# One hybrid encoder block on one core: one wait removed, and several steps of VectorE, ScalarE and TensorE reordered

## The chip, the cores and the metric

The kernel runs on one core of a Trainium2 chip. The metric is the device time of one execution in microseconds (us). Before the change three runs took 961.53 to 962.06 us, median 961.74 us.

## The reference, cut to what matters

One input, x (512 tokens by 1024 channels), is RMS-normalised and multiplied by one large input projection. Three branches use slices of it: A, a chunkwise mLSTM with 4 heads; B, sparse attention, in which an indexer scores all keys for each query and the best 128 are attended by 8 heads; M, cross-attention into 256 memory tokens with 4 heads. Each branch is gated, projected, merged with sigmoid gates and projected once more.

```python
kv_m = rms_norm(mem, mem_norm_g) @ w_mem_kv             # start of the kernel
score = (relu(qi . ki / 8) * wi).sum(heads)             # indexer of branch B
score = where(admissible, score, -inf)
_, idx = lax.top_k(score, 128)                          # top_k = min(256, S // 4)
s = q . k[idx] / sqrt(128); p = softmax(s); o = p @ v[idx]
y_b = o * silu(z_b)
merged = g0 * (y_a @ w_branch[0]) + g1 * (y_b @ w_branch[1]) + g2 * (y_m @ w_branch[2])
out = x + merged @ w_out
```

## The kernel before, in words

**Precision.** Every float32 operand of a large product is split into a high part (a rounded copy made by ScalarE) and a low part (the remainder, made by VectorE with one subtraction); TensorE then runs three passes, high by high, high by low and low by high. So each block of weights has a cast on ScalarE (`split_hi`, `b_high`) and a subtraction on VectorE (`split_lo`, `b_low`) before TensorE may use it. All engines run written-out programs of their own and meet through semaphores; within an engine the order is exactly the order of the code.

**The start.** SP, the queue that issues the loads, sends alternately tiles of `mem` (`load_mem`) and pieces of the first weight panel (`load_piece`). After memory half 0, piece 0, memory half 1 and piece 1 it waits until memory half 0 has landed (`mem_landed[0]`), and goes on with pieces 2, 3 and 4.

**Top-k.** Query tile 0 needs no selection. For tiles 1, 2 and 3 VectorE takes the 8 largest scores of each row and replaces them, 16 times per tile: one such round is `top_round(t)` (MAX8 and MATCH_REPLACE8). The rounds fill VectorE's time from the M stage to the first head pair of B. In all, four rounds of tile 1 and eight of tile 2 stand behind the last panel of M. `make_masks` then turns the marked scores into an additive mask for attention.

**Branch B, head pairs.** `b_unit(i)` on TensorE computes queries, keys and values of head pair i for all tokens with a Strassen-like scheme of seven products (`b_product`, numbers 0 to 6), each 24 matmuls, accumulating in four PSUM banks. VectorE empties or combines banks with `b_add(i, 1)`, `b_add(i, 3)` and `b_add(i, 5)`, each two additions that raise `u_added`; ScalarE saves others with `b_save` and, after product 6, with `b_last_copy`, which raises `u_read`. Product 6 accumulates in banks 0 and 1 and waits at each for the matching half of `b_add(i, 3)` (`u_added`, 6i + 3 and 6i + 4). Then come two `f_panel`s, whose first block in bank 0 waits for `u_read`, that is for `b_last_copy`. On ScalarE `b_last_copy(i)` stands behind `b_values_high(r)`, which waits for all six additions of the pair (`u_added`, 6i + 6). GpSimd squares queries and keys (`b_squares`) behind the same six additions. VectorE's `b_rotary` sums those squares, applies the rotation and raises `b_rotated`, for which the transposes `b_turn_qk` wait. With r = 2i and l = 2i + 1 for the two heads of the pair, head r is attended within the two f_panels and head l within the next pair's unit. VectorE's order is `b_body`, ScalarE's the `b_body` of its own.

**The tail of B.** For the last pair both heads are attended in the first three of four branch panels (`branch_panel(q)`, 8 blocks or slots each: four banks for the first half of K, four for the second). The hooks of a slot (a step of attention) run before that slot's matmuls and before its wait for the bank. Panel q + 1 may write bank b only when VectorE has read what panel q left there: `branch_merge(q, b)` raises `bank_empty[b]`. The chain of one head is `b_turn_qk` (TensorE), `b_qk_high` (ScalarE), `b_qk_low` (VectorE), `b_score` (TensorE), `b_maxes` (VectorE), `b_exps` (ScalarE), `b_scale_p` (VectorE), `b_turn_p` (TensorE), `b_probs_high` (ScalarE), `b_probs` (VectorE), `b_values` (TensorE), `b_finish` (VectorE).

Lines used below: `top_round` L2392, `make_masks` L2468, `b_low` L2483, `b_add` L2490, `b_rotary` L2526 to L2543, `b_values_low` L2555, `b_qk_low` L2547 and L2549, `b_finish` L2522, `branch_merge` L2668, `yb_low` L2661, `m_rest` L2431, `b_high` L1691, `b_values_high` L1719, `z_evac` L1750, `b_squares` L3055, `b_turn_qk` L1094, `b_score` L1105, `b_turn_p` L1113, `b_values` L1123, `b_product` L1141, panels L781.

## Time and profile before

| what | value |
|---|---|
| median of 3 runs | 961.74 us |
| the profiled execution, its own time | 962.06 us |
| its span in the trace | 960.0 us |
| TensorE matmuls busy | 954.0 us (99%) |
| VectorE busy | 707.4 us (74%) |
| ScalarE busy | 535.2 us (56%) |
| GpSimd busy | 346.1 us (36%) |

Times in rows are microseconds from the span's start. PE is TensorE, DVE VectorE, ACT ScalarE, POOL GpSimd, SPq the queue of SP. A busy TensorE is not one at its peak, since its matmuls overlap; the share of 99% says that it hardly ever stood still.

### The profile page before, as it was taken

The numbers are of one execution on the slowest core, as the hardware profiler recorded it, in microseconds if no ns is written. First come the engines' busy times: TensorE is split into PE (matmuls) and PEld (weight loads), VectorE is DVE, ScalarE is ACT, GpSimd is POOL, SyncE is SP. The second block draws the span as 40 slices with busy tenths as digits, with TensorE's granted clock in tenths as the row PEclk, the third lists the DMA queues.
The fourth block names the chain that finished last, engine by engine and source line by source line (L and its number), as shares of the span: only waits on it lengthen the run. The fifth ranks groups of instructions, "written<-read, shape, count | busy, mean of one in ns | idle before, by whom it ended". The sixth has DMA issues, their size and how long they took to land.

```text
span 960.0 us, 13409 instructions
## 1 busy us (share of the span) xinstructions
PE 954.0 (99%) x4897; PEld 839.3 (87%) x4897; DVE 707.4 (74%) x1079; ACT 535.2 (56%) x810; POOL 346.1 (36%) x247
## 2 busy tenths in 40 slices
PE   9999999999999999999999999999999999999998
PEld 7888888888989988988988888898998989988887
DVE  6878987688996676686687565895766958634586
ACT  6877644465456456546573422585765857732251
POOL 0200834456327137136120081362714527107500
PEclk9999999999999999999999999999999999999999
DMA  8624222144531531531354335616043150738312
GB/s 283 245 88 132 89 88 73 58 132 132 166 97 56 176 111 43 155 112 64 121 207 153 122 110 163 221 34 197 1 138 93 33 154 1 258 92 312 125 45 87
DMA packets 105156, 119.27 MB, mean 124 GB/s; under 512 B 4772, under 2 KB 80136, under 8 KB 104332
## 3 DMA queue, kind: packets, MB, share of 16 engines
q1 hardware_dynamic: 105084, 118.53, 38.1%
q8 instruction: 34, 0.56, 0.2%
q14 instruction: 22, 0.18, 0.1%
q10 hardware_dynamic: 16, 0.00, 0.0%
HBM read 106.45 MB, written 12.07 MB: 123 GB/s over the span
## 4 chain that ended last, share of the span: by engine, by line
PE 95%; DVE 3%; DMA 1%; ACT 1%; issue 1%; SPq 0%; DVEq 0%; ACTq 0%
PE proj L781 42%; PE proj L1141 12%; PE proj L1290 9%; PE att L1311 7%; PE proj L1311 5%; PE att L1361 3%; PE proj L951 2%; PE att L1105 2%; PE att L1123 2%; PE att L1070 1%; PE proj L1247 1%; PE att L1113 1%; PE att L1048 1%; PE att L1094 1%; DVE score L2397 1%; PE att L1247 1%
## 5 line engine op out<-in xcount | busy, mean ns | idle before, releaser
L781 PE MATMUL proj<-hT_hi,w_hi 128*128 128x512 f32 x328 | 129.0, 393 | 0.0
L781 PE MATMUL proj<-hT_hi,w_lo 128*128 128x512 f32 x328 | 128.0, 390 | 0.0
L781 PE MATMUL proj<-hT_lo,w_hi 128*128 128x512 f32 x328 | 127.8, 390 | 0.0
L2132 DVE TENSOR_TENSOR w_lo<-w_raw,w_hi 128x2048 fp32r<-128x2048 f32 x28 | 68.5, 2447 | 52.9 <-ACT w_hi L1411 48.9
L1411 ACT ACTIVATE w_hi<-w_raw 128x2048 fp32r<-128x2048 f32 x28 | 53.6, 1914 | 73.2 <-PE proj L781 71.7
L781 PE MATMUL proj<-y_hi,w_hi 128*128 128x512 f32 x192 | 75.2, 392 | 0.7 <-ACT arena L1750 0.7
L781 PE MATMUL proj<-y_hi,w_lo 128*128 128x512 f32 x192 | 74.8, 390 | 0.0
L781 PE MATMUL proj<-y_lo,w_hi 128*128 128x512 f32 x192 | 74.7, 389 | 0.0
L781 PEld LDWEIGHTS proj<-hT_hi,w_lo 128*128 128x128 f32 x328 | 61.6, 188 | 13.1
L781 PEld LDWEIGHTS proj<-hT_lo,w_hi 128*128 128x128 f32 x328 | 61.6, 188 | 12.3
L781 PEld LDWEIGHTS proj<-hT_hi,w_hi 128*128 128x128 f32 x328 | 61.6, 188 | 12.2
L3024 POOL TENSOR_TENSOR w_raw<-merged,w_raw 128x384 f32<-128x384 f32 x32 | 36.2, 1167 | 54.3 <-DVE w_lo L2483 31.6
L2726 DVE TENSOR_TENSOR w_lo<-w_raw,w_hi 128x1536 fp32r<-128x1536 f32 (+1 forms) x21 | 35.9, 1709 | 21.9 <-ACT w_hi L1919 21.9
L1919 ACT ACTIVATE w_hi<-w_raw 128x1536 fp32r<-128x1536 f32 (+1 forms) x21 | 29.1, 1385 | 40.6 <-DMA w_raw<-w_in_in 12.9
L3096 POOL TENSOR_TENSOR w_raw<-merged,w_raw 128x384 f32<-128x384 f32 x32 | 40.3, 1307 | 29.5 <-DVE w_lo L2726 29.5
L781 PEld LDWEIGHTS proj<-y_hi,w_hi 128*128 128x128 f32 x192 | 36.1, 188 | 8.5 <-ACT sig L1750 1.1
L781 PEld LDWEIGHTS proj<-y_hi,w_lo 128*128 128x128 f32 x192 | 36.0, 188 | 7.5
L781 PEld LDWEIGHTS proj<-y_lo,w_hi 128*128 128x128 f32 x192 | 36.1, 188 | 7.4
L2738 DVE SCALAR_TENSOR_TENSOR negmask<-proj,small,negmask 128x511 f32<-128x511 f32 (+2 forms) x48 | 35.5, 747 | 4.0 <-ACT negmask L1952 2.8
L1290 PE MATMUL proj<-hT_hi,w_hi 128*128 128x512 f32 x96 | 37.7, 392 | 0.0
L1290 PE MATMUL proj<-hT_hi,w_lo 128*128 128x512 f32 x96 | 37.4, 390 | 0.0
L1290 PE MATMUL proj<-hT_lo,w_hi 128*128 128x512 f32 x96 | 37.4, 390 | 0.0
(522 smaller groups left out, 2924.0 us busy)
## 6 DMA issues: line engine op xcount, KB each, us to landing
w_raw<-w_in_in SPq DMA_DIRECT2D x36, 512.0 KB, 4.5
w_raw<-w_in_in SPq DMA_DIRECT2D x56, 256.0 KB, 3.7
w_raw<-w_branch_in SPq DMA_DIRECT2D x10, 1024.0 KB, 7.6
merged<-w_in_in SPq DMA_DIRECT2D x38, 256.0 KB, 3.7
merged<-w_in_in SPq DMA_DIRECT2D x14, 512.0 KB, 5.9
w_raw<-w_in_in SPq DMA_DIRECT2D x6, 1024.0 KB, 5.3
w_raw<-w_mem_kv_in SPq DMA_DIRECT2D x10, 512.0 KB, 6.8
yF<-x_in SPq DMA_DIRECT2D x8, 512.0 KB, 7.5
```

The lines of the kernel that those rows point to most:

```text
L781: ins = mm(ps, lhs[a](k, k0), rhs[b](k, k0), start=(first and k == 0 and j == 0), stop=(last and k == KH - 1 and j == 2))
L1141: ins = mm(to[t][:, 0:UNIT_N], lhs[a](k, t), w[b][:, k, :], start=(start and k == 0 and j == 0), stop=(k == KH - 1 and j == 2), skip_group ...
L1290: ins = mm(banks[b][:, :], w[a][:, k, e * P:(e + 1) * P], hT[b_][:, kh * KH + k, :], start=(kh == 0 and k == 0 and j == 0), stop=(kh == 1 ...
L1311: ins = mm(to[t][:, 0:UNIT_N], lhs[a](k, t), w[b][:, k, :], start=(start and k == 0 and j == 0), stop=(k == KH - 1 and j == 2), skip_group ...
L1361: ins = mm(to[t][:, :], lhs[a](k, t), w[b][:, k, :], start=(start and k == 0 and (a, b) == (0, 0)), stop=(k == KH - 1 and (a, b) == parts[ ...
L1411: A_(w_hi[:, kh, :, 0:n], w_raw[:, kh, :, 0:n], ACT.Copy).then_inc(w_hi_done, 1)
L1919: A_(operand(op_hi, n), raw_of(n, first), ACT.Copy).then_inc(op_high, 1)
L2132: V.tensor_tensor(w_lo[:, kh, :, 0:n], w_raw[:, kh, :, 0:n], w_hi[:, kh, :, 0:n].bitcast(F32), ALU.subtract).then_inc(w_lo_done, 1)
L2726: V.tensor_tensor(operand(op_lo, n), raw_of(n, first), operand(op_hi, n).bitcast(F32), ALU.subtract)\
L2738: ins = V.scalar_tensor_tensor(acc[:, lag:], u[:, 0:S - lag], hcw[:, CONV - 1 - lag, b:b + 1], acc[:, lag:], ALU.mult, ALU.add)
L3024: ins = G.tensor_tensor(b_w[out][:, at], b_w[left][:, at], b_w[right][:, at], op)
L3096: ins = G.tensor_tensor(dst[:, at], left[:, at], right[:, at], ALU.subtract)
```

## The change

On SP the wait for memory half 0 goes. On TensorE the attention hooks of the tail move to earlier slots. On ScalarE `b_probs_high` moves ahead of the next panel's cast for both heads, and one cast moves behind `b_qk_high(l)`. On VectorE, two rounds of tile 2 ahead of `m_rest` and two ahead of pair 0 go, and four more stand within pair 0: one more ahead of `b_low(4)`, and four ahead of `b_add(0, 3)` where one stood behind it; `make_masks` moves ahead of `b_add(0, 5)`; `b_values_low(r)` of the last pair moves up; the order of the tail changes. On GpSimd one wait of `b_squares` names `b_rotated` in place of `b_vlow`.

```diff
             load_mem(1)
             load_piece(1, 0, 0)
-            sp.wait_ge(mem_landed[0], 16)
             load_piece(2, 0, 0)
...
-            branch_panel(0, y_split(1), {1: [lambda: b_score(r)], 6: [lambda: b_turn_p(r)]})
-            branch_panel(1, None, {0: [lambda: b_values(r)], 1: [lambda: b_turn_qk(l)], 3: [lambda: b_score(l)],
-                                   6: [lambda: b_turn_p(l)]})
-            branch_panel(2, y_split(2), {0: [lambda: b_values(l)]})
+            branch_panel(0, y_split(1), {1: [lambda: b_score(r)], 5: [lambda: b_turn_p(r)], 7: [lambda: b_values(r)]})
+            branch_panel(1, None, {0: [lambda: b_turn_qk(l)], 2: [lambda: b_score(l)], 5: [lambda: b_turn_p(l)],
+                                   7: [lambda: b_values(l)]})
+            branch_panel(2, y_split(2))
...
             b_exps(r)
+            b_probs_high(r)
             split_hi(GB[0] + 1, 0, GB[1] + 2, 512)
-            b_probs_high(r)
-            split_hi(GB[0] + 1, 1, GB[1] + 2, 512, (3, GB[2][3] + 1))
             b_values_high(l)
             b_qk_high(l)
+            split_hi(GB[0] + 1, 1, GB[1] + 2, 512, (3, GB[2][3] + 1))
             b_exps(l)
+            b_probs_high(l)
             split_hi(GB[0] + 2, 0, GB[1] + 3, 512)
-            b_probs_high(l)
...
-                rounds(2, 1)
+                rounds(2, 2)
                 b_low(n + 4)
...
                 if i:
                     b_finish(tail)
+                rounds(2, 4)
                 b_add(i, 3, (banks[0], banks[1]), b_fifth, 5)
-                rounds(2, 1)
                 b_low(n + 7)
+                if i == 0:
+                    make_masks()
                 b_add(i, 5, (banks[2], banks[3]), b_second, 3)
                 b_low(n + 8)
                 b_rotary(r)
+                b_values_low(r)
                 if last:
                     return
-                b_values_low(r)
-                if i == 0:
-                    make_masks()
...
             b_low(0)
-            for _ in range(2):
-                top_round(2)
             m_rest(M_HEADS - 1)
             bs_low_of(3, 4)
             b_low(1)
-            for _ in range(4):
+            for _ in range(2):
                 top_round(2)
...
             split_lo(GB[0], 0, 512)
-            b_values_low(r)
             b_qk_low(r)
+            b_rotary(l)
             split_lo(GB[0], 1, 512)
             b_maxes(r)
             for k in range(4, KT):
                 ym_low(k)
-            b_rotary(l)
             b_scale_p(r)
+            b_probs(r)
             split_lo(GB[0] + 1, 0, 512)
-            b_probs(r)
+            b_finish(r)
+            b_values_low(l)
+            b_qk_low(l)
             for b in range(4):
                 branch_merge(0, b)
             split_lo(GB[0] + 1, 1, 512)
-            b_finish(r)
-            b_values_low(l)
-            b_qk_low(l)
             b_maxes(l)
             b_scale_p(l)
+            b_probs(l)
             split_lo(GB[0] + 2, 0, 512)
-            b_probs(l)
-            for b in range(2):
-                branch_merge(1, b)
+            b_finish(l)
             for k in range(KH):
                 yb_low(k)
-            for b in range(2, 4):
+            for b in range(4):
                 branch_merge(1, b)
             split_lo(GB[0] + 2, 1, 512)
-            b_finish(l)
...
-                    pool.wait_ge(b_vlow, a)
+                    pool.wait_ge(b_rotated, a)
```

## Rows read from the trace of the kernel before

**Rows 1.** The page: busy time, and the granted clock in 40 slices.

```profile
PE 954.0 (99%) x4897; PEld 839.3 (87%) x4897; DVE 707.4 (74%) x1079; ACT 535.2 (56%) x810; POOL 346.1 (36%) x247
...
PEclk9999999999999999999999999999999999999999
```

**Rows 2.** Waits of TensorE: for whom, us in total, times, longest.

```profile
PE proj L781 <- ACT arena L1750: 0.7, 1, 0.7
PE proj L951 <- ACT w_hi L1462: 0.6, 1, 0.6
```

**Rows 3.** SP's waits up to 30 us; then ScalarE's timeline (start, duration).

```profile
SPq L519 <- DMA merged<-mem_in: 1.0, 1, 1.0
...
7.68 0.63 ACT L1462 ACTIVATE w_hi<-w_raw 128x512 fp32r<-128x512 f32 x1 [2.08 <-DMA w_raw<-w_mem_kv_in]
```

**Rows 4.** Timeline of VectorE, from the end of M to the first pair.

```profile
226.77 0.69 DVE L2431 TENSOR_TENSOR yF<-att,arena 128x512 f32<-128x512 f32 x1 [0.75 <-PE att L1070]
...
232.99 0.55 DVE L2395 MAX8 small<-score 128x8 f32<-128x384 f32 x1
...
237.98 1.76 DVE L2483 TENSOR_TENSOR w_lo<-w_raw,w_hi 128x1536 fp32r<-128x1536 f32 x1
239.66 0.42 DVE L2395 MAX8 small<-score 128x8 f32<-128x256 f32 x1
...
243.59 1.83 DVE L2483 TENSOR_TENSOR w_lo<-w_raw,w_hi 128x1536 fp32r<-128x1536 f32 x1
...
251.68 3.43 DVE L2483 TENSOR_TENSOR w_lo<-merged,w_hi 128x1536 fp32r<-128x1536 f32 x2
255.03 1.01 DVE L2490 TENSOR_TENSOR merged<-proj,merged 128x384 f32<-128x384 f32 x2
255.96 0.55 DVE L2395 MAX8 small<-score 128x8 f32<-128x384 f32 x1
```

**Rows 5.** Timeline of ScalarE in the first pair.

```profile
235.76 1.49 ACT L1691 ACTIVATE w_hi<-w_raw 128x1536 fp32r<-128x1536 f32 x1
...
260.07 0.40 ACT L1719 ACTIVATE b_vh<-yF 128x256 fp32r<-128x256 f32 x1
...
260.69 0.49 ACT L1703 ACTIVATE arena<-proj 128x384 f32<-128x384 f32 x1
```

**Rows 6.** TensorE in the first pair: its timeline, then the chain of waits.

```profile
258.42 0.33 PE L1141 MATMUL proj<-w_hi,hT_hi 128*128 128x384 f32 x1
...
233.52 29.22 PE proj L1141 x168
...
270.94 0.87 PE att L1094 x8
```

**Rows 7.** Timeline of GpSimd, first pair.

```profile
259.97 1.04 POOL L3055 TENSOR_TENSOR arena<-yF 128x512 f32<-128x512 f32 x1 [16.16 <-DVE yF L2490]
```

**Rows 8.** Timeline of VectorE behind the first pair's additions.

```profile
263.56 1.22 DVE L2526 TENSOR_REDUCE small<-arena 128x8 f32<-128x1024 f32 x1 [0.94 <-POOL arena L3055]
...
268.75 0.69 DVE L2541 TENSOR_TENSOR arena<-arena,small 128x512 f32<-128x512 f32 x1
...
270.37 0.17 DVE L2469 MEMSET negmask<- 128x128 f32 x1
...
273.26 1.76 DVE L2483 TENSOR_TENSOR w_lo<-merged,w_hi 128x1536 fp32r<-128x1536 f32 x1
```

**Rows 9.** The chain of waits in the tail: start, us, what.

```profile
523.05 2.79 PE proj L781 x12
525.84 0.87 PE att L1094 x8
```

**Rows 10.** Timeline of VectorE in the tail.

```profile
517.04 1.28 DVE L2668 TENSOR_TENSOR merged<-proj,tabs 128x512 f32<-128x512 f32 x2
...
527.61 0.68 DVE L2549 TENSOR_TENSOR b_kl<-att,b_kh 128x512 fp32r<-128x512 f32 x1
...
545.93 2.49 DVE L2661 TENSOR_TENSOR y_lo<-yF,y_hi 128x512 fp32r<-128x512 f32 x4
```

## The prediction, made before the changed kernel was run

> **What bounds the kernel now.** I read the page's busy times first: TensorE's matmuls cover 954.0 of 960.0 us, while VectorE, the next, covers 74% [rows 1]. Then TensorE's waits: the only two that this change could reach are 0.7 us, before the first branch panel, and 0.6 us, at the start [rows 2]. So TensorE's own program is the bound, in order and all but gapless. Two things follow. A reordering can gain at most about 1.5 us, whatever it does for other engines. And every us for which TensorE is newly made to stand is a us at the end, because nothing later gives it back. The question is therefore not what the moved steps cost, but whether any of them now arrives after TensorE needs it. I walk the new orders through with the durations of the timelines, stage by stage.
>
> **The start.** SP stood 1.0 us for memory half 0 [rows 3]. Without that, pieces 2 to 4 go out up to 1.0 us sooner. What TensorE waits for there is piece 1, issued before the wait either way; ScalarE casts it at 7.68 after 2.08 us of waiting for its landing [rows 3]. The removal can help piece 1 by nothing direct; the sooner transfers may disturb it or, if the transfers behind it let the group finish sooner, spare the stall. Bounds: below, the whole 0.6 us stall goes, with some 0.2 us of small gaps beside it; above, piece 1 is later by the whole 1.0 us by which its successors are sooner, and by as much again through memory half 1, +2.0 us. I take 0: the 256 KB in question is already on its way. The Trainium skill (DMA: Bandwidth & Descriptors, Queues, rings and completion order) says that each transfer engine takes up the descriptors of one ring in order, but that a later one may finish first. By the first half of that the removal costs 0; no row shows the order within a ring.
>
> **The first pair, VectorE.** Four rounds of tile 2 take 4.99 us (232.99 to 237.98), 1.25 each; four rounds of tile 1 take 3.93 us (239.66 to 243.59); one `b_low` takes 1.68 us (two in 3.35, 251.68 to 255.03); the two halves of a `b_add` 0.93 us (255.03 to 255.96) [rows 4]. The change shifts rounds from where VectorE would only wait to where it is late. The two rounds ahead of `m_rest` go, but `m_rest` waits for TensorE until 226.77 anyway [rows 4], so the time is lost and 232.99 stays. From there: two rounds, to 235.48. `b_low(2)` needs ScalarE's cast, which ends at 235.76 + 1.49 = 237.25 [rows 5]: another 1.8 us idle. `b_low(2)` to 238.97, four rounds of tile 1 to 242.90, `b_low(3)` to 244.6, `b_add(0, 1)` to 245.5, two rounds to 248.0, `b_low(4)` to 249.7, two rounds to 252.2, `b_low(5)` and `b_low(6)` to 255.5. Up to here TensorE just gets what it needs: the seven products take 29.22 us, 4.17 each, and the last starts at 258.42 [rows 6], so product 4 at 250.1 and product 5 at 254.26 find their operands 0.3 us ready. Now four rounds, 4.99 us, stand ahead of `b_add(0, 3)`: 260.5. Its first half ends at 261.05. Product 6 wants it at 258.42. **First stall: 261.15 - 258.42 = 2.7 us.**
>
> **Behind it.** `b_add(0, 3)` ends at 261.45, `b_low(7)` at 263.1. `make_masks` now stands here: 273.26 - 270.37 = 2.9 us [rows 8], to 266.0; then `b_add(0, 5)`, its last half landing at 267.0 (before: 259.9, which released ScalarE at 260.07 [rows 5]). ScalarE's `b_values_high(0)` waits for that, and `b_last_copy(0)` is queued behind it: 0.62 us of copies (260.07 to 260.69), then 0.49 [rows 5], to 268.2. The f_panel's first block needs bank 0 from that copy. It wanted to start when product 6 ends, at 258.42 + 4.17 + 2.7 = 265.3, and starts at 268.3. **Second stall: 3.0 us.** GpSimd's squares start with the same addition: 267.1 in place of 259.97 [rows 7]; they then took until 263.56 [rows 7, 8], so 3.6 us, to 270.7. The rotation takes from 263.56 to 268.75 + 0.69 = 269.44 [rows 8], 5.9 us, so `b_rotated` comes at 276.6. The transposes, at 270.94 before [rows 6], are due at 276.6 too. I add 0.1 us. VectorE then has 2.9 us less left to do than before, since the masks are made, and stays ahead. Later pairs have the same orders as before, except that GpSimd's squares of head l start about 0.9 us sooner: nothing waits for them. Stage sum +5.8 us. Bounds: if the rounds ran 10% faster and every semaphore cost nothing, about 1.5 us less; if `b_low(8)`, which runs beside the squares, slows them as it did at its worst, and products 4 and 5 are late as well, 1 us more.
>
> **The tail, head r.** `b_values_low(r)` moving up by 5 us and `b_rotary(l)` moving ahead of the second half of the panel's split delay that split and `ym_low(4)` to `(7)` to about 508.7. The fifth slot of panel 0 needs them at 509.2: hidden with 0.5 us to spare, and a loss of at most as much if GpSimd's squares, now at the same time, slow VectorE. `b_turn_p(r)` and `b_values(r)`, one slot sooner (2.7 us), find probabilities and their low parts ready by about 2 us. But the merges of panel 0 have moved. Before, VectorE did them from 517.04 [rows 10], ahead of panel 1 at 523.05 [rows 9]. Now they stand behind `b_qk_low(l)`, which waits for ScalarE's copies of `b_turn_qk(l)`, which TensorE does only in the first slot of panel 1, at 523.05. Bank 0 is needed right after those transposes. From the rows of before: transposes at 525.84 [rows 9], VectorE's last `b_qk_low` at 527.61 and its next instruction 0.6 us on, 528.2 [rows 10]: 2.4 us. Add a merge, 0.69, and the signal: 3.15 us after the transposes' start, of which they take 0.87. **Third stall: 2.3 us.**
>
> **The tail, head l.** The merges of panel 1 now stand behind `b_finish(l)` and four `yb_low`. `b_values(l)` is the hook of the last slot, so its result is there 2.74 us before panel 2 wants bank 0. Behind it VectorE does `b_finish` (0.6), four `yb_low` (2.4 us by [rows 10]) and one merge (0.69): 3.75 us with the signal. **Fourth stall: 1.1 us.** The 0.7 us wait for `z_evac` [rows 2] stays: nothing ahead of it on ScalarE changes. Bounds of the two together: nothing, if an operand I think late comes early, to 4.5 us, if `b_scale_p` or the split of panel 2 is late too.
>
> **Sum.** 0 + 2.7 + 3.0 + 0.1 + 2.3 + 1.1 = 9.2 us. The profiled execution took 962.06 us (960.0 of it span), 0.3 above the median of 961.74. 962.06 + 9.2 = 971.3, and at the median's level 970.9 us, 1.0% slower.
>
> **Rivals.** First, **only one of the two places stalls.** If the tail's order works out (the ready times there rest on a longer walk), 970.9 - 3.4 = 967.5 us. If the first pair's works out, 970.9 - 5.8 = 965.1 us. For the first speaks the length of the walk, against it that a bank's wait behind a hook in the same slot can't be early. Chance of one of them 0.14.
>
> Second, **everything is covered, and the start gains.** VectorE arrives at `b_add(0, 3)` before 258.3, which takes 2.2 us off my walk, and at `b_add(0, 5)` before 264, and the merges come before 523. Then only the start is left, -0.6 us, or 961.1 us: no change. The point that decides is the 4.99 us of rounds against the 2.9 us that lie between `b_low(6)` at 255.5 and product 6 at 258.42. The rows leave no room for it: 0.04.
>
> Third, **the clock falls behind the stalls.** The granted clock is 2.4 GHz in all forty slices [rows 1], behind its 0.7 us wait too [rows 2]. Stalls of 2.7 and 3.0 us with 4.2 us of work between them are new, and no row shows what the clock does then. If it fell to 1.2 GHz for as long as one product (4.2 us at full speed), the product would take 4.2 us more: 975.1 us. Chance 0.07. The Trainium skill (TensorE: Matmul & The Clock Gate, Part 1: The HAM clock gate) says that the array falls to half its clock after idling and has to earn it back; the rows of before neither show nor exclude it for such gaps.
>
> Fourth, **the start gets worse** by the upper bound of 2.0 us through shared transfers, the rest as forecast: 972.9 us. Chance 0.08.
>
> **How the numbers follow.** The forecast has 0.67: 970.9 us, its own range 969 to 972.5. The range to hold 8 in 10 goes from 967 us (the tail works out) to 973.5 us (a bad start and a little more). A measurement can't tell less than 0.2% (1.9 us) from no change. Faster by more would need more than TensorE waits now: 0.01. Within 0.2%: 0.04, the second rival. Slower: 0.95.
>
> **What would show it.** TensorE's waits should list `proj` L1141 for VectorE's `b_add` (2.7 us, near 258), `proj` L781 for ScalarE near 265 (3.0 us), and `proj` L781 for VectorE's `branch_merge` twice in the tail, 2.3 us behind the transposes and 1.1 us at panel 2. TensorE's busy time should stay at 954 us. The prediction is wrong if the span grows by less than 4 us, or if the stalls stand elsewhere than at these four.

## The result, and the profile after

The changed kernel took 974.37 us (median of 4 runs, 972.04 to 976.38) against 961.75 (961.53 to 962.06) for the kernel before in the same session: a ratio of 1.013, with a 95% interval of 1.0107 to 1.0153. It is 12.6 us slower. The forecast was 9.2 us slower, 970.9 us; 974.37 lies above its whole range.

In the kernel after, lines of the functions above stand one to six lower than before: `b_product` L1140, panels L780, `b_add` L2489, `branch_merge` L2665, `b_low` L2482, `ym_low` L2654, `split_lo` L2131, `b_last_copy` L1702, `make_mask` (within `make_masks`) L2399, `b_values_low` L2554, `b_squares` L3049.

Its profiled execution took 974.56 us, of which 972.5 are span. From the page (busy time; clock in 40 slices), against [rows 1]:

```profile
PE 957.4 (98%) x4897; PEld 840.3 (86%) x4897; DVE 715.0 (74%) x1079; ACT 534.5 (55%) x810; POOL 341.4 (35%) x247
...
PEclk9999999999999999999999999999999999999999
```

The same 4897 matmuls, 3.4 us more of busy time, and 9 us more of standing still. The slices of 24 us hide what the clock did: their line is the same as that of the kernel before. TensorE's waits, which answer to [rows 2] (for whom, us in total, times, longest):

```profile
PE proj L780 <- DVE merged L2665: 3.3, 2, 2.2
PE proj L1140 <- DVE merged L2489: 2.8, 1, 2.8
PE proj L950 <- ACT w_hi L1461: 1.6, 1, 1.6
...
PE proj L780 <- DVE w_lo L2131: 1.4, 1, 1.4
PE proj L780 <- ACT arena L1702: 1.1, 1, 1.1
PE proj L780 <- DVE y_lo L2654: 0.4, 1, 0.4
PE proj L1140 <- DVE b_op_lo L2482: 0.2, 1, 0.2
```

Four of them are the four stalls that were forecast, at the places that were forecast: 2.8, 1.1, and the 3.3, which is 2.2 and 1.05. Of another size or new are 1.6 at the start (0.6 before), the 1.1, where 3.0 was forecast, 1.4 + 0.4 at the tail's first panel, where 0.7 of [rows 2] has gone, and 0.2 at product 4 of the first pair.

The start of TensorE's first long run of matmuls, in the kernel before and after:

```profile
8.36 0.50 PE L951 MATMUL proj<-w_hi,y_hi 128*128 128x512 f32 x1 [0.60 <-ACT w_hi L1462]
9.29 0.50 PE L950 MATMUL proj<-w_hi,y_hi 128*128 128x512 f32 x1 [1.58 <-ACT w_hi L1461]
```

The landmarks in TensorE's timeline after (start, duration, idle time before and for whom). 262.72 answers to 258.42 of [rows 6], 529.99 to 525.84 of [rows 9]:

```profile
262.72 0.41 PE L1140 MATMUL proj<-w_hi,hT_hi 128*128 128x384 f32 x1 [2.77 <-DVE merged L2489]
...
268.18 0.47 PE L780 MATMUL proj<-hT_hi,b_op_hi 128*128 128x512 f32 x1 [1.05 <-ACT arena L1702]
...
502.44 0.47 PE L780 MATMUL proj<-y_hi,w_hi 128*128 128x512 f32 x1 [1.38 <-DVE w_lo L2131]
...
515.92 0.47 PE L780 MATMUL proj<-y_hi,w_hi 128*128 128x512 f32 x1 [0.37 <-DVE y_lo L2654]
...
529.99 1.03 PE L1093 MATMUL att<-ident,arena 128*128 128x128 f32 x8
533.26 0.50 PE L780 MATMUL proj<-y_hi,w_hi 128*128 128x512 f32 x1 [2.23 <-DVE merged L2665]
533.60 0.39 PE L780 MATMUL proj<-y_lo,w_hi 128*128 128x512 f32 x1
...
534.84 0.63 PE L780 MATMUL proj<-y_hi,w_hi 128*128 128x512 f32 x1
535.27 0.63 PE L780 MATMUL proj<-y_lo,w_hi 128*128 128x512 f32 x1
...
563.04 0.47 PE L780 MATMUL proj<-y_hi,w_hi 128*128 128x512 f32 x1 [1.05 <-DVE merged L2665]
```

From 534.84 the matmuls start every 0.43 us instead of every 0.23. The granted clock of this stretch in 2 us steps (window; busy times of PE, PEld, DVE, ACT, POOL; then PEclk):

```profile
532.00:534.00 2.00, 0.74 (x3) 0.65 (x4) 2.00 (x5) 1.57 (x1) 0.00 (x0) 1.00 0.00 0
534.00:536.00 2.00, 2.00 (x7) 1.57 (x7) 2.00 (x3) 0.00 (x0) 0.00 (x0) 0.66 0.00 0
536.00:538.00 2.00, 2.00 (x6) 1.52 (x6) 1.19 (x1) 0.00 (x0) 0.00 (x0) 0.50 0.04 8
538.00:540.00 2.00, 2.00 (x10) 1.64 (x9) 0.00 (x0) 0.00 (x0) 0.00 (x0) 0.99 0.69 217
```

0.50 is the lower of the two levels, 1.2 GHz; 1.00 is the upper one, 2.4 GHz. Behind the 2.2 us wait the clock stood there for about 3.4 us ((1.00 - 0.66) x 2 / 0.5 + 2.0), in which 1.7 us of work was lost. Behind the 2.8 us wait of the same execution it stayed at 1.00.

The 12.5 us of span then come from: start +0.9 (the first long run of matmuls at 9.29 instead of 8.36); first pair +4.75 (the transposes at 276.62, in the chain of waits, instead of 270.94 [rows 6], less the 0.9; the waits of 2.8, 1.1 and 0.2 with their restarts make it up); the tail's first panel +1.2 (waits of 1.4 and 0.4 in place of 0.7, and one restart more); third stall 2.2 + 0.2; clock 1.7; fourth 1.1 + 0.2. That is 12.25; 0.25 is spread over small gaps. The 0.2 behind a wait is its restart. The second matmul starts 0.25 to 0.34 us after the first, where 0.17 and 0.23 are the rhythm; and a wait is counted from the end of the matmul before it, while in the rhythm the next one starts 0.16 us ahead of that end (0.39 - 0.23).

### The profile page after: what moved, and what is told of

Read it like the earlier page. It is cut to its first block, busy times and chain, and to the rows that moved or that the text cites. A ratio compares the mean times of both kernels' runs of the same rounds, so it can differ in the third digit from the quotient of the medians.

```text
span 972.5 us, 13407 instructions
## 1 busy us (share of the span) xinstructions
PE 957.4 (98%) x4897; PEld 840.3 (86%) x4897; DVE 715.0 (74%) x1079; ACT 534.5 (55%) x810; POOL 341.4 (35%) x247
## 4 chain that ended last, share of the span: by engine, by line
PE 87%; DVE 8%; issue 2%; ACT 1%; DMA 1%; POOL 0%; SPq 0%; DVEq 0%; ACTq 0%
PE proj L780 39%; PE proj L1289 9%; PE proj L1140 9%; PE att L1310 7%; PE proj L1310 5%; PE att L1360 3%; PE proj L950 2%; PE att L1122 2%; PE att L1104 1%; DVE score L2396 1%; PE att L1069 1%; DVE small L2394 1%; PE proj L1246 1%; PE att L1112 1%; PE att L1047 1%
## 5 line engine op out<-in xcount | busy, mean ns | idle before, releaser
L780 PE MATMUL proj<-hT_hi,w_hi 128*128 128x512 f32 x328 | 129.0, 393 | 0.0
L780 PE MATMUL proj<-hT_hi,w_lo 128*128 128x512 f32 x328 | 128.0, 390 | 0.0
L780 PE MATMUL proj<-hT_lo,w_hi 128*128 128x512 f32 x328 | 127.8, 390 | 0.0
L2131 DVE TENSOR_TENSOR w_lo<-w_raw,w_hi 128x2048 fp32r<-128x2048 f32 x28 | 68.9, 2462 | 49.6 <-ACT w_hi L1410 45.6
L780 PE MATMUL proj<-y_hi,w_hi 128*128 128x512 f32 x192 | 76.1, 397 | 5.0 <-DVE merged L2665 3.3
L780 PE MATMUL proj<-y_hi,w_lo 128*128 128x512 f32 x192 | 75.4, 393 | 0.0
L780 PE MATMUL proj<-y_lo,w_hi 128*128 128x512 f32 x192 | 75.4, 393 | 0.0
L780 PEld LDWEIGHTS proj<-hT_hi,w_lo 128*128 128x128 f32 x328 | 61.6, 188 | 13.1
L780 PEld LDWEIGHTS proj<-hT_lo,w_hi 128*128 128x128 f32 x328 | 61.7, 188 | 12.3
L780 PEld LDWEIGHTS proj<-hT_hi,w_hi 128*128 128x128 f32 x328 | 61.6, 188 | 12.2
L1918 ACT ACTIVATE w_hi<-w_raw 128x1536 fp32r<-128x1536 f32 (+1 forms) x21 | 29.1, 1385 | 40.5 <-DMA w_raw<-w_in_in 11.6
L3018 POOL TENSOR_TENSOR w_raw<-merged,w_raw 128x384 f32<-128x384 f32 x32 | 32.3, 1040 | 53.2 <-DVE w_lo L2482 29.7
L3090 POOL TENSOR_TENSOR w_raw<-merged,w_raw 128x384 f32<-128x384 f32 x32 | 40.3, 1303 | 29.5 <-DVE w_lo L2720 29.5
L780 PEld LDWEIGHTS proj<-y_hi,w_hi 128*128 128x128 f32 x192 | 36.4, 189 | 13.8 <-issue 4.0
L780 PEld LDWEIGHTS proj<-y_hi,w_lo 128*128 128x128 f32 x192 | 36.5, 190 | 7.8
L780 PEld LDWEIGHTS proj<-y_lo,w_hi 128*128 128x128 f32 x192 | 36.5, 190 | 7.4
```

What stands on the lines that cost most here:

```text
L780: ins = mm(ps, lhs[a](k, k0), rhs[b](k, k0), start=(first and k == 0 and j == 0), stop=(last and k == KH - 1 and j == 2))
L1918: A_(operand(op_hi, n), raw_of(n, first), ACT.Copy).then_inc(op_high, 1)
L2131: V.tensor_tensor(w_lo[:, kh, :, 0:n], w_raw[:, kh, :, 0:n], w_hi[:, kh, :, 0:n].bitcast(F32), ALU.subtract).then_inc(w_lo_done, 1)
L3018: ins = G.tensor_tensor(b_w[out][:, at], b_w[left][:, at], b_w[right][:, at], op)
L3090: ins = G.tensor_tensor(dst[:, at], left[:, at], right[:, at], ALU.subtract)
```

## The experiments

All times are medians of device times, each ratio with its 95% interval against the kernel before on the same chip (961.65 to 961.72 us in the four sessions). "Before +" means the kernel before with only that edit, "after +" the changed kernel with it.

### Which part costs what: b_start, b_pair, b_tail

**b_start**, before + only SP's wait gone:

```diff
             load_piece(1, 0, 0)
-            sp.wait_ge(mem_landed[0], 16)
```

> The kernel before with only the wait for memory half 0 taken away. My theory, from the two traces: the wait of TensorE for piece 1 grows from 0.6 to 1.6 us because pieces 2 to 4, issued 1.0 us sooner, share the transfer engines with piece 1; time +0.9 us (962.7), and piece 1 needs 6.4 us from issue to landing in place of 5.5. Rival: the later landing was chance of that one execution, time within 0.3 us of before.

Measured: 962.88 us, 1.0008 [0.9999, 1.0017]. The interval holds no change by a hair, and the ratio gives 0.8 us where the medians differ by 1.2. In the profile piece 1 is cast at 8.50 instead of 7.68, the first long run starts at 9.18 instead of 8.36, and the span is 0.7 us longer.

**b_pair**, before + only VectorE's edits in and ahead of pair 0:

```diff
-                rounds(2, 1)
+                rounds(2, 2)
                 b_low(n + 4)
...
+                rounds(2, 4)
                 b_add(i, 3, (banks[0], banks[1]), b_fifth, 5)
-                rounds(2, 1)
                 b_low(n + 7)
+                if i == 0:
+                    make_masks()
```

> The kernel before with only VectorE's changes around the first head pair (rounds and masks). My theory: TensorE waits 2.8 us for the first half of b_add(0, 3) and 1.1 us for b_last_copy(0), and the first pair's chain is 4.8 us late, time 966.5. By my prediction's step the second wait would be 3.0 us and the time 967.5. Rival: these waits exist only since the start is late by 0.9 us and the loads with it; then less than 3 us.

Measured: 966.76 us, 1.0058 [1.0044, 1.0071]. In the profiled execution the 2.8 us wait is there and the 1.1 us wait is not. Its clock in 5 us steps says why:

```profile
260.00:265.00 5.00, 3.95 (x16) 3.98 (x17) 4.90 (x11) 0.00 (x0) 0.00 (x0) 0.73 0.15 35
265.00:270.00 5.00, 5.00 (x24) 4.45 (x23) 3.07 (x3) 2.97 (x5) 3.48 (x2) 0.93 0.84 230
```

Here the low clock came behind the 2.8 us wait. It stretched product 6 by 1.7 us, and in that time `b_last_copy` arrived. The expected time, 966.5, came out although one of its two waits did not: the clock had taken its place.

**b_tail**, before + only the tail's edits (all hunks of the tail in the diff above, `b_values_low(r)` among them).

> The kernel before with only the edits of the tail (hooks, ScalarE's and VectorE's order, b_values_low of the last pair, GpSimd's wait). My theory: waits of 1.4 (in place of 0.7), 0.4, 2.2 and 1.1 us, so +4.7 us in waits and the matmuls that restart behind them, and a stretch of some 3.4 us at the lower clock behind the 2.2 us wait, another 1.7 us: 966.5 without and 968.2 with it. Rival: the clock falls only since the first pair has stalled TensorE before; then every execution shows 966.5 and a granted clock of 1.000.

Measured: 966.91 us, 1.0055 [1.0041, 1.0069], with waits of 3.3 (two), 1.4 and 0.4 us. Its profiled execution was the slowest of the five (968.69), and has two more waits that neither other profile has, 1.2 us near 32 and 0.4 near 47, far ahead of the tail; what brings them isn't shown. Four of its five executions had a mean clock of 1.000, so the tail costs about 5 us without any help of the clock: 1.2 + 2.4 + 1.3 by the profile of after. The three parts add up to 1.2 + 5.1 + 5.3 = 11.6 of 12.6 us; the rest, 1.0 us, is less than one low stretch of the clock costs, and whether it is that isn't shown.

### The tail's first panel: a_vlow, a_place

The forecast had the second half of the split and `ym_low` at 508.7, wanted at 509.2, and the first half in time. The first half came late by 1.4 us, and `ym_low` at the fifth slot by 0.4. VectorE in the tail after (start, duration):

```profile
494.95 1.31 DVE L2554 TENSOR_TENSOR b_vl<-yF,b_vh 128x256 fp32r<-128x256 f32 x1
496.19 1.25 DVE L2554 TENSOR_TENSOR b_vl<-merged,b_vh 128x256 fp32r<-128x256 f32 x1
497.37 2.48 DVE L2654 TENSOR_TENSOR y_lo<-merged,y_hi 128x512 fp32r<-128x512 f32 x4
499.78 2.28 DVE L2131 TENSOR_TENSOR w_lo<-w_raw,w_hi 128x2048 fp32r<-128x2048 f32 x1
```

and GpSimd at that time:

```profile
494.94 2.22 POOL L3049 TENSOR_TENSOR arena<-arena 128x512 f32<-128x512 f32 x2 [2.53 <-DVE arena L2540]
```

Each half of `b_values_low` takes 1.3 us instead of 0.42. Rival theories: the two engines get into each other's way, or the instructions are slow at this place. **a_vlow** is after + the old wait of the squares:

```diff
-                    pool.wait_ge(b_rotated, a)
+                    pool.wait_ge(b_vlow, a)
```

> The changed kernel with GpSimd's b_squares waiting for b_vlow again. My theory: in the last pair b_values_low took 2.4 us in place of 0.75 since GpSimd's squares ran beside it; without that, VectorE's split for panel 0 is 1.7 us sooner, TensorE's wait of 1.4 us there becomes the 0.7 us for z_evac, time 0.7 to 0.9 us below the changed kernel's median (973.5). Rival: the slow b_values_low comes from something else (its place in VectorE's queue), nothing changes.

Measured: 972.93 us, 1.0119 [1.0103, 1.0134]; the expectation of a shorter wait was missed: it stayed at 1.3 us. VectorE's timeline:

```profile
494.07 0.43 DVE L2554 TENSOR_TENSOR b_vl<-yF,b_vh 128x256 fp32r<-128x256 f32 x1
494.41 0.42 DVE L2554 TENSOR_TENSOR b_vl<-merged,b_vh 128x256 fp32r<-128x256 f32 x1
494.75 4.18 DVE L2654 TENSOR_TENSOR y_lo<-merged,y_hi 128x512 fp32r<-128x512 f32 x4
```

`b_values_low` is fast again (0.43 and 0.42 us), and the four `ym_low`, now beside the squares (495.00 to 497.78), take 4.18 us where they took 2.48. The delay is of the two engines together; the wait only chose who paid.

**a_place** is a_vlow + `b_values_low(r)` of the last pair back in the tail:

```diff
                 b_rotary(r)
-                b_values_low(r)
                 if last:
                     return
+                b_values_low(r)
...
             split_lo(GB[0], 0, 512)
+            b_values_low(r)
             b_qk_low(r)
```

> The changed kernel with GpSimd's wait on b_vlow and b_values_low(r) of the last pair back behind the first split of panel 0, so that the squares of head l run beside no two-input VectorE work on SBUF. My theory after a_vlow, where the 1.7 us only moved to the four ym_low: these, the split and b_values_low(r) then take their plain 2.4, 2.2 and 0.75 us, the split comes 2.4 us sooner, TensorE's wait of 1.4 us becomes the 0.7 us for z_evac: time 0.7 to 0.9 us below the changed kernel. Rival: GpSimd's overlap is no cause, the wait stays at 1.3 to 1.4 us.

Measured: 973.29 us, 1.0119 [1.0102, 1.0136], 1.1 us less than after. The 1.4 us wait is gone and the 0.7 us wait for `z_evac` back; four `ym_low` take 2.50 us, since the squares start only behind `b_values_low`. So by the waits the place of `b_values_low(r)` was worth 0.7 us. The medians can't tell it: with four runs that spread over 1.7 us a_place is 1.1 us below after and 0.4 above a_vlow. The 0.4 us wait at the fifth slot stays in both; in a_place VectorE stood 1.05 us for the squares, which now come late, ahead of `b_rotary(l)`, so what that wait would be without the squares isn't shown.

### The masks: a_masks, a_masks2, b_masks

The second stall was forecast at 3.0 us with 2.9 us for `make_masks` [rows 8]. After, it took 1.2 us (264.68 to 265.88):

```profile
264.68 0.17 DVE L2468 MEMSET negmask<- 128x128 f32 x1
264.88 0.90 DVE L2399 TENSOR_SCALAR negmask<-score 128x256 f32<-128x256 f32 x3
...
265.88 1.02 DVE L2489 TENSOR_TENSOR yF<-proj,yF 128x384 f32<-128x384 f32 x2
```

Of the kernel before, the row that [rows 8] left out, and GpSimd's at the same time:

```profile
270.57 2.59 DVE L2400 TENSOR_SCALAR negmask<-score 128x256 f32<-128x256 f32 x3
```

```profile
270.56 2.31 POOL L3055 TENSOR_TENSOR arena<-arena 128x512 f32<-128x512 f32 x2 [3.48 <-DVE b_vl L2555]
```

**a_masks** is after + the masks back at their old place:

```diff
-                if i == 0:
-                    make_masks()
                 b_add(i, 5, (banks[2], banks[3]), b_second, 3)
...
                 if last:
                     return
+                if i == 0:
+                    make_masks()
```

> The changed kernel with make_masks back behind b_values_low(r) of the first pair. My theory: the masks took 1.2 us ahead of b_add(0, 5) and 2.9 us only where GpSimd's squares run beside them. Without them there, b_last_copy(0) is 1.2 us sooner and TensorE's wait of 1.1 us for it goes; behind the rotation the masks or b_values_low take up to 2 us longer again beside the squares. Time 1.1 to 1.3 us below the changed kernel's 974.4. Rival, my prediction's step (the masks cost 2.9 us wherever they stand): 2.9 us or more below.

Measured: 974.24 us, 1.0121 [1.0104, 1.0138]. The wait for `b_last_copy` is gone, yet the time is not less. ScalarE's timeline shows that the masks were its cause: the first half of `b_last_copy` ends 4.05 us after product 6 has started (268.51 and 264.46), where it takes 5.31 in after (267.56 + 0.47, and 262.72), and product 6 takes 4.17. But here the clock fell behind the 2.8 us wait, and that stretched product 6 to 5.80 us, the same as in b_pair, a_vlow and a_place, where the masks stand at their new place and the 1.1 us wait is missing too. In after, with the wait and no slow clock there, the f_panel starts 5.46 us behind product 6. So in an execution whose clock falls there the masks cost nothing, and the low stretch costs only some 0.3 us more than the wait that it takes the place of. The mean clock of the profiled execution was 0.995: there were three low stretches (0.71 at 10 to 15 us, 0.66 at 265 to 270, 0.66 at 535 to 540), and the one of its four executions with a mean clock of 1.000 took 971.56 us. The masks still took 0.90 us at the old place, since `b_values_low` (1.31 + 1.26), ahead of them, met the squares, as it does in after. **a_masks2**, a_masks + the old wait of the squares (as in a_vlow), tells whether it was the place or the neighbour:

> The kernel a_masks (changed kernel, masks back behind b_values_low(r)) with GpSimd's wait on b_vlow again, so that the squares start with the masks. My theory, contention of VectorE and GpSimd: the masks take 2.9 us as in the kernel before, and b_values_low(r) 0.75 us in place of 2.5; time as a_masks. Rival: the masks are faster in the changed kernel for a reason of their own and keep their 1.2 us.

Measured: 973.88 us, 1.0127 [1.0112, 1.0143], and in VectorE's timeline:

```profile
273.75 0.42 DVE L2554 TENSOR_TENSOR b_vl<-yF,b_vh 128x256 fp32r<-128x256 f32 x1
274.10 0.42 DVE L2554 TENSOR_TENSOR b_vl<-merged,b_vh 128x256 fp32r<-128x256 f32 x1
274.49 0.17 DVE L2468 MEMSET negmask<- 128x128 f32 x1
274.69 2.58 DVE L2399 TENSOR_SCALAR negmask<-score 128x256 f32<-128x256 f32 x3
```

The same three instructions, 2.58 us with the squares beside them (274.68 to 276.99) and 0.90 without, at the same place. **b_masks** takes the step alone, before + the masks ahead of `b_add(0, 5)`:

```diff
                 b_low(n + 7)
+                if i == 0:
+                    make_masks()
                 b_add(i, 5, (banks[2], banks[3]), b_second, 3)
```

> The kernel before with only make_masks moved ahead of b_add(0, 5). My theory: 1.2 us there, b_last_copy(0) starts at 261.8 and frees bank 0 at 262.3, before the f_panel wants it at 262.6; b_rotated comes at 270.6, wanted at 270.9: time as before, within 0.3 us. Rival, the step of my prediction (2.9 us): bank 0 at 264.0 and b_rotated at 272.3, so 1.4 us slower.

Measured: 961.74 us, 1.0000 [0.9991, 1.0009]; masks 0.90 us, no new wait of TensorE. Moving the masks is free by itself. On top of the rounds it brings the 1.1 us wait, in an execution whose clock stays high there.

### The rounds: a_rounds

After + the four rounds behind the addition:

```diff
-                rounds(2, 4)
                 b_add(i, 3, (banks[0], banks[1]), b_fifth, 5)
+                rounds(2, 4)
```

> The changed kernel with the four rounds of tile 2 behind b_add(0, 3) in place of ahead of it. My theory: TensorE's 2.8 us wait at product 6 goes, but VectorE reaches b_add(0, 5) no sooner, so ScalarE's b_last_copy(0) comes at the same time and the whole wait, some 4.4 us, stands before the first f_panel block: time within 0.5 us of the changed kernel. Rival (each wait has its own cause): 2.8 us less.

Measured: 976.53 us, 1.0162 [1.0145, 1.0179]. The 2.8 us wait is gone and this one has come:

```profile
PE proj L780 <- ACT arena L1702: 4.1, 1, 4.1
```

5 us of rounds moved from one side of `b_add(0, 3)` to the other stay ahead of `b_add(0, 5)`, and the stall moves to where that one is waited for: 4.1 instead of 2.8 + 1.1. The expectation of the same time within 0.5 us was missed by the median, 2.2 us above after, with intervals that overlap. The mean clocks, 0.993 to 0.998 (0.9953 in the mean, 0.9970 in after; each 0.001 is 1 us), account for 1.7 of it. The cost is in the number of rounds ahead of the pair's last addition, not in their place.

### The merges: a_merge

After + the four `branch_merge(0, b)` ahead of `b_finish(r)`:

```diff
             split_lo(GB[0] + 1, 0, 512)
+            for b in range(4):
+                branch_merge(0, b)
             b_finish(r)
             b_values_low(l)
             b_qk_low(l)
-            for b in range(4):
-                branch_merge(0, b)
```

> The changed kernel with the four branch_merge(0, b) ahead of b_finish(r). My theory: the 2.2 us wait of panel 1 behind the transposes goes, the one of 1.1 us at panel 2 stays: 2.3 us less, 972.1, and in executions where the clock fell behind that wait another 1.7 us less. Rival: b_qk_low(l), now behind the merges, is late instead and TensorE waits the same time at b_score(l).

Measured: 969.74 us, 1.0081 [1.0065, 1.0098], 4.6 us less than after. Its only wait for merges is the fourth:

```profile
PE proj L780 <- DVE merged L2665: 1.0, 1, 1.0
```

2.2 + 0.2 us of wait and 1.7 us of clock are gone, 4.1 together; near 530 the matmuls run at 0.23 us each. From the transposes of head l to the end of the span the two profiled executions take 442.5 us (after, from 529.99) and 438.3 (from 530.62): 4.2 less. In that execution of after a stall forecast at 2.3 us was worth nearly twice that, because the clock fell behind it. It doesn't always: of the seven profiled executions with the 2.2 us wait the clock fell behind it in four (after, a_place, a_masks, a_masks2), and not in a_vlow, a_rounds and b_tail.

The profiled execution of a_merge shows something else too. Behind its 2.8 us wait the clock was low for 6.8 us (0.59 at 261 to 262, 0.50 in each us from there to 268), twice as long as in the others; its f_panel starts 7.05 us behind product 6 instead of 5.46.

### What a stall costs: c_short, c_long

Two waits made on purpose ahead of the last branch panel, for casts that are done a few us late there:

```diff
-            branch_panel(3, None)
+            branch_panel(3, None, {0: [lambda: pe.wait_ge(w_hi_done, 2 * (GB[0] + 3) + 2)]})
```

c_long waits for `w_lo_done` instead.

> The kernel before, with TensorE made to wait once, ahead of branch panel 3 (a stretch without any other wait), until ScalarE has cast the panel's second half: one clean wait of 2.0 us (cast 1.92 us behind the end of panel 2). My theory: such a wait costs itself and 0.2 us for the matmuls that restart, 963.9, and in some executions a stretch at the lower clock behind it, 1.7 us more. Rival: the clock falls only where several waits lie close together; then every execution shows a granted clock of 1.000 and 963.9.

> The same with the wait ended by VectorE's subtraction behind the cast, so one wait of 4.3 us (1.92 + 2.3 + signals). My theory: 4.5 us for the wait and, now in every execution, 1.7 us of lower clock: 967.9, granted clock 0.998. Rival: 966.2 at 1.000.

Measured: c_short 965.82 us, 1.0040 [1.0024, 1.0055], for one wait of 2.1 us. Its clock:

```profile
574.00:576.00 2.00, 0.92 (x2) 0.83 (x3) 1.97 (x2) 0.98 (x1) 2.00 (x1) 0.73 0.41 125
576.00:578.00 2.00, 2.00 (x6) 1.53 (x5) 1.97 (x3) 0.00 (x0) 1.92 (x2) 0.50 0.16 16
```

In this execution (966.40 us) 2.1 + 0.2 + 1.7 = 4.0 of 4.7 us. Two of four had a mean clock of 0.998 (966.40 and 965.88), two of 1.000 (965.75 and 964.55). So the four don't separate cleanly by the clock; its 1.7 us is read from the profile. c_long took 972.98 us, 1.0121 [1.0105, 1.0136]. Its wait was 8.8 us where 4.3 was expected: I had overlooked that VectorE's split stands behind the merges of panel 2. The clock was low from about 575 to 585, some 6 us of it in the wait (which began at 572.6), where it costs nothing, and 4 us (581.3 to 585.3) behind it, which cost 2.0: 8.8 + 2.0 + 0.2 of 11.3 us. All four executions had a mean clock of 0.995.

The mean clocks of all runs show how often the clock was low anywhere in an execution. With a wait of 2.1 or 2.2 us as the longest (c_short, b_tail) 3 of 9 executions were below 1.000; with the 2.8 us wait, in most with the 2.2 us one as well (b_pair, after, a_vlow, a_place, a_masks, a_masks2, a_merge), 29 of 30; with 4.1 us (a_rounds) all 4; with 8.8 all 4; with none of them (b_start, b_bank, b_masks, b_swap, s_late) none of 55. Where it fell only the profiled executions tell: behind the 2.8 us wait in six of seven (not in after), behind the 4.1 us wait, behind the 2.2 us wait in four of seven. One low stretch, in a_masks from about 9.5 to 12.9, stands behind a start wait of only 1.3 us.

### The start, and the wait that was there before: b_swap, s_late, b_bank

```diff
-            load_mem(1)
             load_piece(1, 0, 0)
+            load_mem(1)
             sp.wait_ge(mem_landed[0], 16)
```

is **b_swap**; **s_late** waits for `piece_landed[0]` in the place of `mem_landed[0]`, which is later.

> The kernel before with weight piece 1 issued ahead of memory half 1. My theory: piece 1 is 0.47 us sooner in the queue and TensorE's 0.6 us wait for its cast shrinks to 0.1 or 0.2 us, while memory half 1, wanted at 7.1 us, still lands in time: 0.4 us faster. Rival: memory half 1 is late instead, same time or slower.

> The kernel before with SP waiting for weight piece 0 in place of memory half 0, so that pieces 2 to 5 are issued some 1.4 us later than before and 2.4 us later than with the change. My theory (sooner successors delay piece 1): piece 1 lands sooner than its 5.5 us from issue, by about as much as it was later in the changed kernel, some 4.6 us, and TensorE's wait for its cast goes; ScalarE then waits 1.4 us longer for pieces 2 and 4, which may cost TensorE up to 1 us. Rival: piece 1's landing does not depend on what is issued behind it, the 0.6 us wait stays and the later pieces come on top.

Measured: b_swap 961.45 us, 1.0002 [0.9993, 1.0011]; s_late 962.09 us, 1.0002 [0.9993, 1.0011]: no difference to be told. In both the wait for piece 1 went, and others of 0.2 and 0.4 us came; the 0.4 us that b_swap was expected to gain did not show. What they do show is when piece 1 lands, read from the start of ScalarE's cast of it. With successors held until piece 0 had landed (s_late, one execution): 6.51. Held until memory half 0 had landed (before, b_pair, b_tail, b_bank, b_masks, c_short, c_long): 6.70 to 7.68, mean 7.3. Not held (b_start, after and the six variants of after): 7.60 to 8.61, mean 8.1. The kernels before and after were each profiled at the late end of their group. Of after, where [rows 3] have 7.68:

```profile
8.61 0.63 ACT L1461 ACTIVATE w_hi<-w_raw 128x512 fp32r<-128x512 f32 x1 [3.03 <-DMA w_raw<-w_mem_kv_in]
```

**b_bank** is before without the early wait on bank 1, whose release comes from `z_evac`; the matmuls' own waits still guard the bank:

```diff
-            pe.wait_ge(bank_empty[1], BF[2][1] + 2 * PAIRS - 1)
```

> The kernel before without TensorE's early wait for bank 1 ahead of the branch panels (the panel's own wait, ahead of the block that writes bank 1, has the same value). The 0.7 us wait ends with ScalarE's evacuation of bank 1, while the first block needs bank 0, free 0.1 us before the f_panel ends. My theory: the wait goes, 0.7 to 0.9 us faster, 960.9, and faster than both kernels. Rival: the next wait of the same chain (the split of the panel's second half, which ScalarE does behind that evacuation) takes its place; no change.

Measured: 961.01 us (960.58 to 961.18, 11 runs), 0.9993 [0.9984, 1.0002]. The 0.7 us wait of [rows 2] is gone, with 0.2 us left at its place, and the span is 958.8 us. All 11 executions lie at or below the lowest of 21 of the kernel before in that session (961.18; in the other sessions single ones went down to 960.79), but the interval of the ratio includes no change. It is the fastest version here: 13.4 us below after and 0.7 us below before, which this measurement just fails to separate from no change.

## Why the prediction was wrong in size and right in kind

Four terms of the sum failed, and together they took the time out of the range: the clock, put at nothing (1.7 us lost in the profiled execution); head r of the tail, put at nothing (1.2 us); the start, put at nothing (0.9 us); and, the other way, the masks at 2.9 us, which took 1.2 and made the second stall 1.1 instead of 3.0.

**The bound.** Right. TensorE's waits and its clock account for the whole change, and the busy time of the other engines for none of it.

**Start, priced at 0 with bounds -0.8 to +2.0.** Wrong within its bounds: +0.9 in the profile; in b_start +0.8 by the ratio and in the profile, +1.2 by the medians, with an interval down to 0. The fourth rival had its kind right, half its size. The step that failed is "the 256 KB in question is already on its way": it was, and still landed 0.8 us later in the mean when its successors were issued sooner. The prediction leaned on the Trainium skill (DMA: Bandwidth & Descriptors, Queues, rings and completion order), by which descriptors of one ring are taken up in order. The landing times above show that this order does not fix when piece 1 lands. The other half of the sentence there, that a later transfer may finish first, is neither shown nor excluded by them.

**First stall, 2.7.** Right: 2.8. The walk had `b_add(0, 3)` start at 260.5; it started at 262.01, of which 0.9 is the start's delay. TensorE was late by as much, so the difference held. That is partly luck: the other 0.6 us on VectorE's side come mostly from `b_low(2)`, 2.23 us long in after where the walk had 1.7, and on TensorE's side from product 4, whose operand the walk had ready 0.3 us early and which waited 0.2 us for it. In a_masks2 `b_low(2)` took 1.76 us and that wait is absent.

**Second stall, 3.0.** Wrong: it was 1.1. a_masks2 and b_masks show why, and a_masks that the wait was the masks' doing. The step that failed is "`make_masks` now stands here: 2.9 us". The duration was read from a row in which GpSimd's squares ran beside it, and was carried to a place where they could not yet have started. The row of that duration was not among [rows 7, 8]; had it been read beside GpSimd's, the two starts, 270.57 and 270.56, would have pointed to it. With the 1.2 us that the masks took in after, the walk gives 3.0 - 1.7 = 1.3. The transposes, forecast at 276.6, did come at 276.62, but by luck: the start was 0.9 us later than forecast, and the first pair about as much shorter.

**The tail, head r: 0 with 0.5 to spare.** Wrong: +1.2. The walk checked the fifth slot and the split's second half; the first half, due at the panel's start, was not walked. Its 1.4 us wait, where 0.7 for `z_evac` was to stay, has two causes, the move of `b_values_low(r)` and the squares beside it (1.7 us more on VectorE): with only the squares moved (a_vlow) it stayed at 1.3, with both undone (a_place) it fell back to 0.7. The fifth slot, where the forecast named a risk of "at most as much" as 0.5 us from the squares, waited 0.4.

The Trainium skill (SBUF — State Buffer, Who interferes with whom) says that a VectorE instruction with two inputs in SBUF, or in a mode that uses both ports, and a GpSimd instruction that reads SBUF exclude each other for a whole instruction. The rows agree: 0.42 us became 1.3 and 0.90 became 2.59, though no row tells in which mode the masks' instructions ran. GpSimd pays as well: in after, `b_low(8)` started first, at 266.81, and took its 1.75 us, and the square beside it took 2.49 us; in the kernel before the squares started first (259.97), and it was `b_low(8)` that took longer, 2.43 us, and then the second square, 2.56 instead of 1.04. And two subtractions of `b_qk_low(r)`, with one input in PSUM, took 0.68 us each in a_place, the second of them within the squares (500.05 to 502.09), as they do without them. By that rule the masks without squares are the cheaper case; by how much, no row of the kernel before tells.

**Third and fourth stall, 2.3 and 1.1.** Right: 2.2 and 1.05, each with 0.2 of restart. a_merge shows the third. The fourth has a slip of 0.1 in its sum: 3.75 - 2.74 is 1.0.

**The clock.** The third rival had 0.07 and the forecast none of it. Its price, 4.2 us, was too high in most cases and its chance much too low. What happened in the profiled execution of after is a stretch of about 3.4 us at 1.2 GHz behind the 2.2 us wait, 1.7 us of loss. By their mean clocks, three of after's five executions had one such stretch (0.998) and two had as much low clock as two or three (0.996, 0.995). That widens the spread, but isn't all of it: the three with 0.998 took 972.04, 974.15 and 974.56 us, and 21 executions of the kernel before in one session, all at 1.000, took 961.00 to 963.80. The reading that failed is "the granted clock is 2.4 GHz in all forty slices, behind its 0.7 us wait too": a row on 0.7 us tells nothing of 2.7, and a slice of 24 us can't show a stretch of 3.4, as the line of after, with the same forty digits, shows.

Against the forecast sum of 9.2, then: start +0.9, first pair 4.75 instead of 5.8, head r +1.2, restarts +0.1 and +0.2 at the third and fourth stall, clock +1.7: 12.25. The 1.9 us too much for the masks hid a part of what was missing elsewhere.

What stays open: whether b_start's +1.2 is wholly the later landing of piece 1 (its profile and the ratio show 0.8), how long a low stretch can last (6.8 us in a_merge), and why the clock fell behind the 2.8 us wait in b_pair's profile and not in that of after.

## What to carry to other kernels

Where TensorE is the bound without gaps, follow every reordered step to the TensorE instruction that waits for it, the first one due and not the tightest one; each us of stall counts, and one near 3 us was followed by a stretch of slow clock, at 1.7 us of lost work or more, in six of seven profiled executions. Before a duration is carried from one place of a timeline to another, look at what the other engines did in that row: 0.90 and 2.59 us are the same three instructions. And fillers such as the top-k rounds are free only up to the next thing that TensorE waits for: moved behind one such step, they stalled it at the next.

## What the hardware did that I had not expected

- VectorE and GpSimd, both on operands in SBUF: three `tensor_scalar` of 128x256 took 0.90 us alone and 2.59 beside the squares; a subtraction of 128x256 0.42 and 1.3; four of 128x512 2.48 and 4.18. The squares too became slower: two took 2.04 us in a_place, 2.22 beside `b_values_low` and 2.78 beside the four subtractions.
- TensorE's clock at the lower level for about 3.4 us behind waits of 2.1 to 4.1 us, and once behind one of 1.3, at a cost of 1.7 us; once for 6.8 us. In c_long it fell during the wait, 2.5 us into it, and rose 4 us behind its end.
- A transfer of 256 KB landed 0.8 us later in the mean when its successors followed without a pause, and 0.8 us sooner, in one execution, when they were held back longer.
- A low stretch can take the place of a later wait: from product 6 to the f_panel it is 5.46 us with the 1.1 us wait (after) and 5.80 with the slow clock and no wait (b_pair, a_place, a_masks).
